# Rearranging the persistent SBUF tiles of a two-block float32 network on one core: the arena moves from the middle to the end

## What is computed

```python
# first_block: for each of two layers, three sub-layers, each on a normed and modulated h
x = x + 0.5 * g * swiglu(h, w_gate, w_up, w_down)       # D_FF = 2816
x = x + g * hybrid_mixer(h, ...)    # layer 0: RG-LRU and chunked SSD
x = x + g * mlstm_block(h, ...)     # layer 1: chunked mLSTM, 4 heads
x = x + 0.5 * g * swiglu(h, w_gate, w_up, w_down)
x = rms_norm(x, final_norm_g)
# second_block
proj = h @ w_in                     # attention, RWKV and gate parts
o_attn, o_rwkv = dilated_attention_mixer(q, k, v, positions), rwkv7_mixer(...)
merged = sigmoid(g_attn) * (o_attn @ wb1) + sigmoid(g_rwkv) * (o_rwkv @ wb2)
x = x + gt1 * rms_norm(merged @ w_out)
x = x + gt2 * rms_norm(square(relu(h @ w_ff1)) @ w_ff2)
```

## Time and profile before

| | |
|---|---|
| three runs | 3568.95 us median (3556.6, 3568.95, 3569.0) |
| profiled execution | 3569.0 us, its span 3567.2 us |
| PE busy | 3435.3 us, 96% of the span |
| weight loads of PE (PEld) | 2789.7 us, 78% |
| DVE (VectorE) | 2019.1 us, 57% |
| ACT (ScalarE) | 1212.8 us, 34% |
| POOL (GpSimd) | 360.7 us, 10% |
| mean granted TensorE clock | 0.98 |
| moved by DMA | 382.75 MB, 107 GB/s on average |

### The profile page before, as it was taken

The page is one execution under the profiler, slowest core; times in us unless marked ns, Lnnn a source line. Parts: engine busy times, 40 slices in busy tenths (PEclk is TensorE's granted clock), DMA queues, the critical chain, the costliest instruction groups (busy, mean ns, idle before and its releaser), DMA issues. The chain is left out here.

```text
span 3567.2 us, 56582 instructions
## 1 busy us (share of the span) xinstructions
PE 3435.3 (96%) x22456; PEld 2789.7 (78%) x22456; DVE 2019.1 (57%) x2820; ACT 1212.8 (34%) x1783; POOL 360.7 (10%) x264
## 2 busy tenths in 40 slices
PE   7999999999999999999999999999988999999998
PEld 4888777878888788876678888877767777888886
DVE  6666666846665666574444433365666773454343
ACT  3222346432222322243243322333434543233231
POOL 1000003410000000010101000130103330010000
PEclk9999999999999999999899999999989999989999
DMA  6554322125554555421033233222210002323332
GB/s 240 194 197 176 126 76 71 54 95 189 188 208 139 183 188 204 161 87 48 1 101 99 89 96 108 91 84 83 65 37 6 7 7 67 95 65 100 94 94 77
DMA packets 103765, 382.75 MB, mean 107 GB/s; under 512 B 11424, under 2 KB 15136, under 8 KB 103200
## 3 DMA queue, kind: packets, MB, share of 16 engines
q1 hardware_dynamic: 103584, 380.15, 31.8%
HBM read 378.01 MB, written 2.10 MB: 107 GB/s over the span
## 5 line engine op out<-in xcount | busy, mean ns | idle before, releaser
L459 PE MATMUL bank<-h_hi,w_hi 128*128 128x512 f32 x2576 | 1015.6, 394 | 29.2 <-DVE w_lo L254 26.4
L460 PE MATMUL bank<-h_lo,w_hi 128*128 128x512 f32 x2576 | 1005.4, 390 | 0.0
L461 PE MATMUL bank<-h_hi,w_lo 128*128 128x512 f32 x2576 | 1005.2, 390 | 0.0
L254 DVE TENSOR_TENSOR w_lo<-w_raw,w_hi 128x1024 fp32r<-128x1024 f32 (+2 forms) x480 | 634.4, 1322 | 387.0 <-ACT w_hi L248 375.9
L248 ACT ACTIVATE w_hi<-w_raw 128x1024 fp32r<-128x1024 f32 (+2 forms) x475 | 521.3, 1097 | 288.2 <-PE bank L461 247.9
L459 PEld LDWEIGHTS bank<-h_hi,w_hi 128*128 128x128 f32 x2576 | 485.0, 188 | 146.9 <-DVE w_lo L254 30.1
L461 PEld LDWEIGHTS bank<-h_hi,w_lo 128*128 128x128 f32 x2576 | 485.0, 188 | 102.4
L460 PEld LDWEIGHTS bank<-h_lo,w_hi 128*128 128x128 f32 x2576 | 485.4, 188 | 100.7 <-issue 1.9
L459 PE MATMUL bank<-f_gu_hi,w_hi 128*128 128x512 f32 x704 | 274.2, 390 | 0.0
L461 PE MATMUL bank<-f_gu_hi,w_lo 128*128 128x512 f32 x704 | 273.9, 389 | 0.0
L460 PE MATMUL bank<-f_gu_lo,w_hi 128*128 128x512 f32 x704 | 273.9, 389 | 0.0
(11 more groups left out here) (645 smaller groups left out, 4773.2 us busy)
## 6 DMA issues: line engine op xcount, KB each, us to landing
ada_tiles<-in_ada SPq DMA_DIRECT2D x180, 512.0 KB, 4.1
w_raw<-in_gu SPq DMA_DIRECT2D x176, 512.0 KB, 4.4
w_raw<-in_dn SPq DMA_DIRECT2D x64, 704.0 KB, 5.0
w_raw<-in_w_ff SPq DMA_DIRECT2D x64, 512.0 KB, 3.6
w_raw<-in_w_hyb SPq DMA_DIRECT2D x36, 512.0 KB, 3.4
w_raw<-in_w_rkv SPq DMA_DIRECT2D x24, 512.0 KB, 3.6
w_raw<-in_w_attn SPq DMA_DIRECT2D x20, 512.0 KB, 3.6
w_raw<-in_w_hout SPq DMA_DIRECT2D x16, 512.0 KB, 3.4
```

What stands on the lines that cost most here:

```text
L254: K.nc.vector.tensor_tensor(K.w_lo[:, half, 0:kb * P], K.w_raw[:, slot, 0:kb * P], K.w_hi[:, half, 0:kb * P].bitcast(F32), ALU.subtract).t ...
L459: nc.tensor.matmul(K.ps[bank][:], wh, hi, start=start, stop=False)
L460: nc.tensor.matmul(K.ps[bank][:], wh, lo, start=False, stop=False)
L461: last_mm = nc.tensor.matmul(K.ps[bank][:], wl, hi, start=False, stop=stop)
```

## The change

Only addresses change. The stretch reserved for the arena (`ARENA_BYTES`) goes; `K.x` and the ring `K.w_raw` are allocated ahead of and behind `h_hi`/`h_lo`, and the arena now begins behind the last persistent tile and may reach to the end of SBUF. The two size assertions compare with that end.

```diff
-ARENA_BYTES = 110 * 1024
...
     K.cols_at, ncols = column_map()
+    K.x = sb("residual", [P, DC, S])
     K.h_at = (K.top[0] + 31) // 32 * 32
     K.h_hi = sb("h_hi", [P, DC, S], F32R)
     K.h_lo_at = (K.top[0] + 31) // 32 * 32
     K.h_lo = sb("h_lo", [P, DC, S], F32R)
-    K.arena = (K.top[0] + 31) // 32 * 32
-    K.arena_end = K.top[0] = K.arena + ARENA_BYTES
+    K.w_raw_at = (K.top[0] + 31) // 32 * 32
+    K.w_raw = sb("w_raw", [P, RING, KB_MAX * P])
     K.w_hi_at = (K.top[0] + 31) // 32 * 32
     K.w_hi = sb("w_hi", [P, SPLIT, KB_MAX * P], F32R)
     K.w_lo_at = (K.top[0] + 31) // 32 * 32
     K.w_lo = sb("w_lo", [P, SPLIT, KB_MAX * P], F32R)
-    K.x = sb("residual", [P, DC, S])
-    K.w_raw_at = (K.top[0] + 31) // 32 * 32
-    K.w_raw = sb("w_raw", [P, RING, KB_MAX * P])
     K.cols = sb("cols", [P, ncols])
...
     K.c_turn = sb("c_turn", [P, ADA_TURNS * DC])
+    K.arena = (K.top[0] + 31) // 32 * 32
...
     K.t = at("h_scaled", [P, DC, S], F32, K.h_lo_at)
-    assert K.top[0] <= nc.sbuf_usable_end, K.top[0] - nc.sbuf_usable_end
+    K.arena = (K.top[0] + 31) // 32 * 32
...
-    assert at[0] <= K.arena_end, at[0] - K.arena_end
+    assert at[0] <= nc.sbuf_usable_end, at[0] - nc.sbuf_usable_end
```

More of the change, by code:

```diff
@@ L2973, in rwkv @@
     pp = [sb(f"pp{x}", [P, NC]) for x in range(2)]
-    assert at[0] <= K.arena_end, at[0] - K.arena_end
+    assert at[0] <= K.nc.sbuf_usable_end, at[0] - K.nc.sbuf_usable_end
     strict, pair_t, pair, causal, eye = (masks[:, n * L:(n + 1) * L] for n in range(5))
```

## The result

The changed kernel takes 3587.44 us (median of 6 runs, 3583.77 to 3594.31) against 3563.82 us for the kernel before (median of 6, 3555.19 to 3569.09): ratio 1.0072, 95% interval 1.0055 to 1.0088 (the quotient of these two medians is 1.0066; the record lists 12 runs of the changed kernel in all, 3581.66 to 3595.47). It is slower by 0.7%, outside the forecast range of 3550 to 3581 us, on the side to which 0.07 had been given.

A forecast was written before the change was run, and what follows sets the result against it. The prediction took TensorE, busy for 96% of the span, to bound the kernel. To the profiled 3569.0 us it added 0 each for instructions, alignment, reads, writes and loads, and forecast 3568 us, range 3550 to 3581.

The forecast's parts named there:

- Instructions, order, waits (0 us): Whole kernel: no instruction, semaphore, DMA or buffer is added, removed or moved in a queue, so 0 us.
- Alignment: 0 us: Persistent tiles move by multiples of 512 bytes, only the arena by 131 x 512 + 192; smaller alignments kept, 0 us.
- TensorE's reads: Moving operands of the 11,616 matmuls against their weights: no dependence on distance, 0 us, bounds -11.6 to +11.6 us.
- The argument from seven placements: Line 459's tiles at seven placements all have a median of 389 ns, so distance to the weights was taken as 0.
- The bound of 1 ns: 1 ns either way on each of 11,616 matmuls, the resolution of the rows: -11.6 to +11.6 us.
- Writers beside the reads, VectorE, ScalarE: Writes next to what TensorE reads, and VectorE's and ScalarE's own operations, cost nothing more after the move: 0 us.
- Loads (0 us): DMA loads into `ada_tiles` and `w_raw`: loads wait for slots, only first loads are exposed, 1.6 us either way; 0 us.
- The slower rival: Around `h_hi`/`h_lo`, `w_raw`, weights and arena: reads and writes now lying together collide; 3615 or 3584 us, chance 0.07.
- its test of 1.5 ns a matmul: Loss per matmul from which collisions of reads and writes would decide: 17.8 us / 11,616.
- its smaller price, 3584 us: 4 ns a matmul only while ScalarE or VectorE work, about a third of the time: 15 us.
- The sign "for the arena's tiles alone": In the changed profile, medians of 390 ns or more on those tiles would show reads wrong and tell which neighbour.
- The faster rival: The old placement cost TensorE something in every matmul, 13.4 ns at most; freeing it gives 156 us, 3413 us; chance 0.03.

The follow-up runs named there:

- the last experiment: The kernel before with `h_lo` moved by 64 bytes and the arena, weights, residual and ring by 256: 3602.76 us, ratio 1.0115.

## Why the prediction was wrong

- **Instructions, order, waits (0 us): right.** There are 56,582 instructions in both, and PE waits 27.8 us on `w_lo` where it waited 28.1.
- **"Alignment: 0 us" failed.** This is the step. It found that the arena alone moves by 192 bytes inside a block of 512 and costed that at nothing, without a row: in the trace of before no two operands of these matmuls stand at such an offset. Measured, it is +24.0 us: 1168 triples of the arena and half of the 128 of `hyb`, 1232 x 3 = 3696 matmuls, at 24.0 / 3696 = 6.5 ns each. What the sum lacked is that the arena's tiles left D = 0 for D = 64 while the weights' own start moved by a multiple of 256.
- **TensorE's reads.** The argument from seven placements looked at distances in kilobytes. They are not even seven places: `f_gu_hi`, `u_hi` and `oa_hi` all begin at the arena's start. And every distance is a multiple of 256, as the four that it gives would have shown (145,408, 112,640, 22,528, and 33,024 for `ml_hi` from the arena's start), so for D they are one case. Their spread bounded nothing about a shift by 192. The bound of 1 ns was the resolution of rows that don't show the changed situation; on the arena's matmuls 6.5 ns came. The bounds were taken for all 11,616 matmuls, where 3696 are what slowed.
- **Writers beside the reads, VectorE, ScalarE: right.** `h_lo` now ends where the DMA writes `w_raw`, and the steps behind `h_hi` and `h_lo` have not changed; `w_lo` has 1225 ns as before, and 64 bytes more undo the loss with all neighbours left in place.
- **Loads (0 us): right for the time.** `ada_tiles` land after 4.3 us where it was 4.1. The rule on 256-byte boundaries from the Trainium skill (DMA: Bandwidth & Descriptors, How a descriptor splits into AXI transactions) would have made that less by 1.5%, an estimate of the prediction's that these rows don't bear out. It describes what a transaction fetches and names no memory; carrying it over to writes into SBUF was the prediction's own step. No wait followed either way.
- **The slower rival.** "Reads and writes that now lie together collide" had the right sign, and its test of 1.5 ns a matmul was passed (24.0 us / 11,616 = 2.1 ns), but the wrong partner: the time follows D, the distance between TensorE's own two operands, which points to its two reads and not to writers; and the place is the arena's whole length, not its border. That its smaller price, 3584 us, is near the 3587 measured is luck: it counted 4 ns in a third of all matmuls. The sign "for the arena's tiles alone" came, but it told the operands' offset and no neighbour. The rival's one piece of evidence set a mean, 393 ns on line 431, against a median, 389; the mean of line 459 on `h_hi` is 394.

```profile
L459 PE MATMUL bank<-h_hi,w_hi 128*128 128x512 f32 x2576 | 1015.6, 394 | 29.2 <-DVE w_lo L254 26.4 <-PEq L104 2.7
```

- **The faster rival,** 13.4 ns in every matmul from the old placement, is not borne out: in no experiment did the pitch fall under 226 to 227 ns, and what makes it more than 213.3 is not known.
- **The Trainium skill** (SBUF — State Buffer, Who interferes with whom) gives TensorE two independent read ports, for the moving operand and for the weights, and says that it never waits on anyone. I let it support a time of 3569. Nothing measured here speaks against it between engines. For the engine's own two operands the experiments say otherwise: their places relative to each other cost 0.7% here and 2.0% with D at 64 throughout. The measurement decides.

What is shown for these matmuls: their steps depend on D, are shortest at 0 modulo 256 and longer at 32, 64, 128 (and 192, `h_lo` in the last experiment), and don't depend on where the pair lies. That the stream of the moving operand and a weight load disturb each other in SBUF is the reading of this, not shown by itself. What stays open: at which moment they meet. Moving `w_lo` alone puts most of the loss behind its own matmul, moving `h_lo` alone spreads it over three; neither fits "own weights" or "next weights" alone. Distances under 32 bytes weren't tried, and whether matmuls of other types lose in the same way was not tried apart.

## What to carry to other kernels

When tiles are rearranged, work out for every matmul of the kind measured here (float32r, 512 columns, a new weight block each) the weights' address minus the moving operand's, modulo 256, before and after, and not only the tiles' own alignment; round the start of a shared region to 256 bytes relative to the weights instead of 32. In a kernel that TensorE bounds, look at its starts or durations by tile: 5 ns on some tiles and none on others pointed to the cause here, and 3696 small losses made this one. Placements that agree in the old trace say something only about what differs between them.

## What the runs showed of the hardware that was not expected

Float32r matmuls of 512 columns, back to back with a new 128x128 weight block each, start every 226.7 ns if D is 0 and every 233.3 ns if D is 64, at a granted clock of 1.00 (354 against 344 or 345 matmuls in 80 us). The weight loads last 188 ns (187 to 188 in median) in both cases, so their duration doesn't show the disturbance. VectorE and ScalarE showed nothing of the kind in any placement tried: the medians of `w_lo` are 1225 or 1226 ns and those of `w_hi` 1050 to 1052 ns in all twelve traces.
